# First stage of a hybrid encoder step: second projection ahead of the sixth tile's turn, and products of constants ahead of the first three turns

## What is computed

```
h = rms_norm(x, ln1);  proj = h @ w_in
q, k, v, f, xr, yg = split(proj)          # 8 heads of 64; f is one number per head and row
q = rms_norm(q, q_gain);  k = rms_norm(k, k_gain)
logf = log_sigmoid(f + b_f)
c = cumsum(logf)                          # per head, along the rows
s = q @ k^T / 8 + c[query] - c[key], causal;  attn = softmax(s) @ v
# a gated linear recurrence on xr, yg; w_out; then an MLP with squared relu
```

## Time and profile before

| | |
|---|---|
| median of 3 runs | 1388.46 us (1388.18 to 1390.19) |
| the profiled execution | 1392.37 us, its span 1390.7 us |
| mean granted clock of PE over the span | 0.994 |
| PE busy | 1351.1 us, 97% |
| DVE busy | 1038.5 us, 75% |
| ACT busy | 529.5 us, 38% |
| POOL busy | 391.4 us, 28% |

### The profile page before, as it was taken

The page is one execution under the profiler, slowest core; times in us unless marked ns, Lnnn a source line. Parts: engine busy times, 40 slices in busy tenths (PEclk is TensorE's granted clock), DMA queues, the critical chain, the costliest instruction groups (busy, mean ns, idle before and its releaser), DMA issues.

```text
span 1390.7 us, 21437 instructions
## 1 busy us (share of the span) xinstructions
PE 1351.1 (97%) x7399; PEld 1171.4 (84%) x7399; DVE 1038.5 (75%) x1610; ACT 529.5 (38%) x980; POOL 391.4 (28%) x397
## 2 busy tenths in 40 slices
PE   5999999999999998999999999999999999999998
PEld 4866948669589996889899999999999999999997
DVE  6775573745736687766888888888888888888885
ACT  6234252332436763324334333433442344234320
POOL 4411101111000030112354235423542453245310
PEclk9999999999999999999999999999999999999999
DMA  6042524324261212121211011102101110121004
GB/s 205 8 122 82 131 62 121 103 80 111 58 171 44 70 45 91 49 76 31 62 61 55 5 60 60 41 19 60 60 30 30 60 60 16 44 60 60 2 29 136
DMA packets 129544, 92.89 MB, mean 67 GB/s; under 512 B 14678, under 2 KB 119126, under 8 KB 129492
## 3 DMA queue, kind: packets, MB, share of 16 engines
q1 hardware_dynamic: 129492, 92.20, 23.0%
HBM read 78.28 MB, written 9.71 MB: 63 GB/s over the span
## 4 chain that ended last, share of the span: by engine, by line
PE 85%; DVE 6%; DMA 3%; ACT 2%; POOL 2%; issue 1%; SPq 1%; DVEq 0%; POOLq 0%; ACTq 0%
PE psum L2147 16%; PE psum L2148 16%; PE psum L2149 16%; PE psum L2644 8%; PE psum L2646 8%; PE psum L2645 8%; PE psum L2410 2%; DMA k_c<-in_cache_k_dram 2%; PE psum L2392 1%; PE psum L2230 1%; PE psum L2395 1%; PE psum L2363 1%; DVE tops L1673 1%; POOL rs L822 1%; DVE cross_qk L1660 1%
## 5 line engine op out<-in xcount | busy, mean ns | idle before, releaser
L2013 DVE TENSOR_TENSOR mix<-mix,psum 128x512 f32<-128x512 f32 x660 | 418.1, 685 | 91.5 <-PE psum L2646 87.2
L2147 PE MATMUL psum<-h_hi,wu_hi 128*128 128x384 f32 x768 | 259.5, 338 | 0.9 <-DVE wu_lo L1978 0.9
L2148 PE MATMUL psum<-h_lo,wu_hi 128*128 128x384 f32 x768 | 258.1, 336 | 0.0
L2149 PE MATMUL psum<-h_hi,wu_lo 128*128 128x384 f32 x768 | 258.1, 336 | 0.0
L2644 PE MATMUL psum<-wd_hi,u_hi 128*128 128x512 f32 x516 | 201.3, 390 | 0.1
L2645 PE MATMUL psum<-wd_lo,u_hi 128*128 128x512 f32 x516 | 200.7, 389 | 0.0
L2646 PE MATMUL psum<-wd_hi,u_lo 128*128 128x512 f32 x516 | 200.7, 389 | 0.0
L2147 PEld LDWEIGHTS psum<-h_hi,wu_hi 128*128 128x128 f32 x768 | 144.3, 188 | 10.0 <-issue 1.3
L2148 PEld LDWEIGHTS psum<-h_lo,wu_hi 128*128 128x128 f32 x768 | 144.3, 188 | 8.7
L2149 PEld LDWEIGHTS psum<-h_hi,wu_lo 128*128 128x128 f32 x768 | 144.4, 188 | 0.0
L1308 ACT CAST wd_hi<-raw 128x512 fp32r<-128x512 f32 x109 | 67.2, 623 | 179.5 <-PE psum L2646 81.1
(11 more groups left out here) (338 smaller groups left out, 2510.9 us busy)
## 6 DMA issues: line engine op xcount, KB each, us to landing
raw<-in_w_up_dram SPq DMA_DIRECT2D x32, 512.0 KB, 6.1
raw<-in_w_down_dram SPq DMA_DIRECT2D x32, 512.0 KB, 4.3
k_c<-in_cache_k_dram SPq DMA_DIRECT2D x32, 256.0 KB, 3.1
raw<-in_w_in_dram SPq DMA_DIRECT2D x32, 192.0 KB, 3.9
out_dram<-mix SPq DMA_DIRECT2D x9, 512.0 KB
v_c<-in_cache_v_dram SPq DMA_DIRECT2D x16, 256.0 KB, 4.4
raw<-in_w_in_dram SPq DMA_DIRECT2D x8, 512.0 KB, 4.1
raw<-in_w_out_dram SPq DMA_DIRECT2D x8, 512.0 KB, 4.2
```

The source lines that it names most:

```text
L2013: nc.vector.tensor_tensor(half_of(t, half), half_of(t, half), psum[:, product_bank(n), :].rearrange("p (k n) -> p k n", n=P), op).then_inc ...
L2147: nc.tensor.matmul(out, hi(k), r_hi(k), start=first and k == 0, stop=False)
L2148: nc.tensor.matmul(out, hi(k), r_lo(k), start=False, stop=False)
L2149: last = nc.tensor.matmul(out, lo(k), r_hi(k), start=False, stop=end and k == n - 1)
```

## The change

PE: 20, 10 and 20 turns of the identity into bank 3 (`warm`) stand ahead of the turns of tiles 0, 1 and 2; nobody reads them. `project(1)` stands right behind the turn of tile 4; what stood between (the turn of the small parameters, the turns of tiles 5 to 8, `forgets(0)` and `forgets(1)`) comes behind it, and the parameters are turned into bank 3 rather than 5. `forgets(2)` moves from behind `project(1)` into `project(2)`, `turn_inputs` from the first to the third quarter of `project(2)`, `turn_qk(0)` behind `project(2)`, `turn_forgets` from `project(3)` into `project(4)`.

DVE: `mean(1)` and `norm(1)` come among the tiles of the first stage; the series of logf is cut in two, with `norm(2)` between; both `prompt_sums` stand behind `norm(3)`, in halves with `prompt_rows`. SP: `keys_out(0, 2)` goes ahead of the rows of sums, which are written and read back in two halves. ACT, POOL: the same order as their new neighbours need.

```diff
@@ sync
-                if p == 0:
-                    sp.wait_ge(c_split, 1)
-                    sp.dma_start(c_dram[:, 0, :], c_row[0:H, :].bitcast(F32)).then_inc(c_saved, 16)
-                    sp.dma_start(c_dram[:, 1, :], c_row[32:32 + H, :].bitcast(F32)).then_inc(c_saved, 16)
-                    sp.wait_ge(c_saved, 32)
-                    sp.wait_ge(operands_set, 2)
-                    decay_rows(0)
...
                 keys_out(p, 2)
+                if p == 0:
+
+                    sp.wait_ge(operands_set, 2)
+                    for half in range(2):
+                        at = slice(half * SPAN, (half + 1) * SPAN)
+                        sp.wait_ge(c_split, half + 1)
+                        sp.dma_start(c_dram[:, 0, at], c_row[0:H, at].bitcast(F32)).then_inc(c_saved, 16)
+                        sp.dma_start(c_dram[:, 1, at], c_row[32:32 + H, at].bitcast(F32)).then_inc(c_saved, 16)
+                        sp.wait_ge(c_saved, 32 * half + 32)
+                        if half == 1:
+                            sp.wait_ge(c_rows_in, 32)
+                        decay_rows(0, at)
@@ vector
+                    if p == 0 and t == 2:
+                        first_stage(4)
+                        past_parts(1)
+                        forget_sizes()
...
-                    if p == 0 and t == 3:
-                        prompt_sums(1)
...
-                    if p == 0 and t == 0:
-                        first_stage(1)
+                    if p == 0 and t < 2:
+                        first_stage(2 * t + 1)
+                    if p == 0 and t == 2:
+                        forget_series()
                     norm(t)
-                    if p == 0 and t == 1:
-                        past_parts(1)
-                        forget_sizes()
+                    if p == 0 and t == 2:
                         forget_values()
-                    if p == 0 and t == 2:
-                        prompt_sums(0)
                     if p == 0 and t == 3:
-                        prompt_rows()
+                        for half in range(2):
+                            prompt_sums(half)
+                            prompt_rows(half)
                         own_sums()
@@ tensor
+            def warm(n):
+
+                for _ in range(n):
+                    nc.tensor.transpose(psum[:, f_bank(1), 0:P], ident[:], ident[:])
+
...
                     for t in range(3):
+                        warm((20, 10, 20)[t])
                         turn(t)
                 if i == 1:
                     turn(3)
                     turn(4)
+                if i == 2:
+                    turn(5)
                     pe.wait_ge(small_in, 16 * SMALL)
...
-                    turn(5)
                     forgets(0)
                     turn(6)
+                    pe.wait_ge(params_copied, 1)
                     forgets(1)
...
                 def amid(t, quarter):
-                    if p == 0 and (t, quarter) == (2, 0):
+                    if p == 0 and (t, quarter) == (2, 1):
+                        forgets(2)
+                    if p == 0 and (t, quarter) == (2, 2):
                         turn_inputs()
-                    if p == 0 and (t, quarter) == (3, 2):
+                    if p == 0 and (t, quarter) == (4, 2):
                         turn_forgets()
...
-                    if p == 0 and t == 1:
-                        forgets(2)
                     if p >= 1:
                         samples_meanwhile(p - 1, t)
-                    if 1 <= t < 8:
+                    if p == 0 and t == 2:
+                        turn_qk(0)
+                    if (1 if p >= 1 else 2) <= t < 8:
                         turn_qk(t - 1)
```

More of the change, by code:

```diff
@@ L862, in _ @@
             for t in range(5, NT):
+                if t == NT - 1:
+                    pair_rstd(0, 1)
                 x_rstd_of(t)
@@ L896, in _ @@
                         pool.wait_ge(shift_zeroed, 2 * p - 1 + hp)
-                for t in range(2 if p == 0 else 0, NT):
+                for t in range(3 if p == 0 else 0, NT):
                     pair_rstd(p, t)
@@ L1482, in first_stage @@
                 if i == 2:
-                    for t in (6, 7):
-                        x_mean_of(t)
-                        turn_lo(t - 2)
-                        x_norm(t)
+                    x_mean_of(6)
+                    turn_lo(4)
+                    x_norm(6)
+                    dve.wait_ge(rows_turned, 1)
+                    nc.vector.tensor_copy(param[:, :, 0:ROWS], psum[:, f_bank(1), 0:LC * ROWS].rearrange(
+                        "p (c r) -> p c r", c=LC)).then_inc(params_copied, 1)
+                    x_mean_of(7)
+                    turn_lo(5)
+                if i == 3:
+                    x_norm(7)
                     x_mean_of(8)
+                if i == 4:
                     x_norm(8)
@@ L1519, in forget_values @@
                 d.link(nc.vector.tensor_scalar(l_f[:], l_q[:], 1.0 / 15, None, ALU.mult))
-                for odd in (13, 11, 9, 7, 5, 3):
+                for odd in (13, 11, 9):
+                    d.link(nc.vector.scalar_tensor_tensor(l_f[:], l_f[:], 1.0 / odd, l_q[:], ALU.add, ALU.mult))
+            def forget_values():
+                for odd in (7, 5, 3):
                     d.link(nc.vector.scalar_tensor_tensor(l_f[:], l_f[:], 1.0 / odd, l_q[:], ALU.add, ALU.mult))
@@ L2352, in bound @@
                         pe.wait_ge(bound_read, 20 * p + BOUND_ORDER.index(BOUND_AFTER[hp, t]) + 1)
+                    if p == 0 and (hp, t) == (0, 1):
+                        pe.wait_ge(c_split, 2)
                     if (hp, t) == (0, 4):
+                        if p == 0:
+                            pe.wait_ge(c_rows_in, 64)
                         pe.wait_ge(lo_done, NT * p + 4)
```

27 lines of the change are left out of this document (12 added, 15 removed).

## The result

| kernel | median (lowest to highest), us | runs | to the kernel before, 95% interval |
|---|---|---|---|
| before | 1388.46 (1386.92 to 1390.19) | 7 | |
| after | 1392.31 (1389.55 to 1394.11) | 7 | 1.0028 [1.0018, 1.0037] |

The change made the kernel slower, by 3.9 us of 1388, clear of the noise but small; forecast was +0.6 us, with 1391.7 us as the end of the range. The profiled execution of the changed kernel took 1394.11 us (span 1392.4), that of before 1392.37 (1390.7).

What follows compares the result with a forecast made beforehand. PE and DVE hand work to and fro, neither alone the bound, with SP's queue third. A schedule shorter by 0.8 us and a clock fall of 1.4 us give +0.6 us: 1389.1 us, range 1384.6 to 1391.7.

Steps and rivals of the forecast that it cites:

- The stores hold `norm(3)`: On DVE, `norm(3)` waits 3.75 us for a key store queued on SP behind nine stores of logf.
- The landing is at 54.15 + 5.9: SP's first key store lands 5.9 us behind logf, at 60.05 us, and `norm(3)` waits for it.
- rival (C): Keys land sooner, so the stores don't hold DVE; `norm(3)` starts at 56.3 us: 1384.0 us, chance 0.17.
- Logf is ready at 54.15 us: On DVE, 27.4 us of work and 2.6 us of waits from 24.15 us make logf 3.1 us earlier.
- none for POOL's roots: DVE's waits for POOL's roots ahead of logf, before 0.72 and 1.55 us, vanish because other work lies between.
- the one for f: DVE waits some 0.65 us for f ahead of logf, because `forgets(2)` needs the lo part of tile 8.
- I take 0 us: The 50 turns of constants ahead of tiles 0 to 2 on PE change the time by 0 us, bounds +0.5 and -0.4.
- Rival (D): Clock falls around `turn(3)`, `project(1)` runs at half speed until some 31 us, logf 2.3 us late: 1391.4 us, chance 0.12.
- The fall behind 65 us: PE pauses 4 us behind `project(5)`, from 65.0 to 69.1 us, and the clock falls: 1.4 us lost, 1.2 to 2.4.
- The 0.3 us from the rows of sums: The first half of the sums is back from DRAM at 67.3 us, ahead of `norm(4)`, saving 0.3 us.
- From `norm(3)` to `norm(4)`: On DVE this stretch grows from 6.26 to 9.05 us by two running sums and rounding in halves.
- The base: The profile of before stood 3.9 us above the median, so +0.6 us was added to the median, 1388.46 us.

Runs made afterwards that it cites:

- Experiment 1: Changed kernel with the three key stores issued ahead of the nine stores of logf: 1387.57 us, 0.9999 of the kernel before.
- all_moves_no_products: Changed kernel without the 50 turns, key stores ahead of logf's, DVE's `qgain` product later, POOL's `e_row` built between the roots of x: 1389.20 us.
- experiment 7: Changed kernel with 16 more turns in two pauses (1390.81 us), with only the first 20 turns (1389.62), and reprofiled (1390.23); mean clocks compared with and without turns.
- after_again: The changed kernel, unchanged, profiled a second time: 1390.23 us (span 1388.5).
- no_products: Changed kernel without the 50 turns of the identity: 1389.07 us, 1.0004 of the kernel before.

## Why the prediction was wrong

The forecast was 1389.1 us in a range up to 1391.7, the time is 1392.31. By steps:

- **The stores hold `norm(3)`: right, and the largest single effect.** "The landing is at 54.15 + 5.9": the 5.9 us measured 5.97 (57.06 to 63.03). The wait was 4.86 us rather than 3.75, because DVE came to the wait 1.1 us behind logf (57.06 to 58.17) and not 2.15: I had counted 1.1 us for POOL's root ahead of the wait, and the root ran during it. Experiment 1 gives the price in time, 4.7 us; rival (C) had put 5.1 on it. This was forecast, so it is no part of the miss.
- **"Logf is ready at 54.15 us": wrong, 57.06,** and by more than the 1 us that the prediction had allowed. This term carries the miss at `norm(4)` (72.19 us, forecast 69.1). The 2.9 us are: 0.24 us later start (24.39 against 24.15); waits of 4.26 us (0.35, 1.57, 1.02, 0.85, 0.47) where I had 2.6, +1.66; and 28.4 us of work (57.06 - 24.39 - 4.26) where I had 27.4, +1.0. Of the waits, those up to the landing of the small parameters were 0.6 us longer (0.35 and 1.57 against 1.3), and I had written "none for POOL's roots" (0.85) and had none for ACT's squares (1.02, which came with the fall at 25 us); the one for f, 0.65, wasn't there. Of the work, `cc` and `c_mid`, moved beside POOL's building of `e_row`, took 3.06 us rather than 1.10. In the kernel before it was the instruction ahead of them that stood there:

```profile
44.56 1.10 DVE L1561 TENSOR_SCALAR c_past<-cc 64x512 bf16<-64x512 f32 x1
```

  It takes 0.42 us in the changed kernel, so that the net is +1.3 us, more than the whole +1.0. In the profiles without the fall at 25 us (`all_moves_no_products` and the kernels with the order of before aside) logf comes at 55.3 to 55.9 us, still 1.1 to 1.8 us late: the fall is 1.2 us of the miss, the rest is in every one of them.
- **"I take 0 us" for the constants' products: the step that failed.** My bounds were -0.4 and +0.5 us. They cost 3.2 us in the changed kernel, 2.6 us in the kernel before, 1.4 and 1.5 us in the two with the keys first. I had looked at what the turns delay, and not at what an earlier rise of the clock leads to. In its place the runs show that with the turns the clock is lower on average, by an estimated 1.1 to 2.1 us of PE's work (experiment 7), while the earlier end of `project(0)` only lengthens waits. One such fall is placed: behind the pauses ahead of tiles 3 and 4, in two of five profiles, and in none of the four of the same order without the turns. Rival (D) had this mechanism at 0.12, with 2.3 us on logf; measured 1.2 us on logf between two executions of one kernel.
- **The fall behind 65 us: right, but dearer in the text than on the chip.** I took 1.4 us. From norm(3) to norm(8) it takes 31.0 to 31.1 us in the seven profiles with the new order in which the clock falls in 70 to 75 us, and 30.3 us in the two in which it never falls in 60 to 80 us. It takes 30.3 us in `after_again` as well, where the fall came earlier, ahead of `norm(4)`:

```profile
60.00:65.00 5.00, 2.35 (x9) 2.33 (x9) 3.00 (x6) 2.05 (x5) 0.00 (x0) 0.76 0.18 44
65.00:70.00 5.00, 3.82 (x19) 3.50 (x18) 4.63 (x13) 1.36 (x4) 1.01 (x1) 0.90 0.08 15
```

  PE waits for `norm(4)` behind `project(5)` anyway, 2.26 us there and 3.79 in the first profile: the slower products took their time out of that wait. So a fall costs 0.8 us there or nothing, by where it lands. The 0.3 us from the rows of sums can't be seen.
- **From `norm(3)` to `norm(4)`** 9.16 us against 9.05: right.
- **The base.** The sum was moved to the median, and that was right: the profile of before had a fall at 304 us that its second profile hasn't (2.4 us of the fourth pair, 0.9 of them the longer wait).

Against the median, then: +0.6 forecast, +3.85 measured. Without the turns the changed kernel is at 1389.07 us: the forecast 1389.1 would have been that kernel's time, but in part by luck, with logf 1.1 us later than forecast and norm(8) 1.2 us later than before where 0.6 were forecast. In the medians, the whole miss is the size of the term that was priced at 0 (3.2 us, from 1389.1 to 1392.31); logf's other 1.1 us must be made good elsewhere, and I didn't find where, beyond the fall behind 65 us that was 0.6 us cheaper and the differences between executions behind norm(8).

**What stays open.** Of the 2.6 to 3.2 us that the turns cost in the kernel before and in the changed one, the traces place only part in the first pair: 0.2 to 0.6 us in the kernel before, and between `after_again` and `no_products` nothing at norm(8) (92.16 and 92.21), though the spans are 1.5 us apart. The traces do show where those 1.5 us arise. At 543.9 us the same products on PE are still 0.3 us apart, and at 547.3 us 1.5: the first kernel's clock falls there and the second's doesn't, behind a pause of 1.53 us in both. Windows of `after_again`, then of `no_products`:

```profile
545.00:550.00 5.00, 5.00 (x18) 3.92 (x18) 3.80 (x5) 1.80 (x4) 1.06 (x2) 0.77 0.02 3
```
```profile
545.00:550.00 5.00, 5.00 (x23) 4.03 (x22) 4.14 (x5) 1.47 (x4) 0.72 (x2) 1.00 0.00 0
```

Whether the turns make that fall more frequent isn't shown: it comes in seven of the eight profiles with all 50 turns and in six of the eight others. So how an act in the first 16 us could lower the mean clock, beyond the fall at 25 us and those behind 60 us, stays open.

Why the turns make the small parameters land later is open too; SP issues its loads within 0.2 us of the same times (the last group at 20.39 us in `after_again`, 20.20 in `no_products`), and that is less than the 0.5 to 1.0 us. One candidate stands in the traces and was not tested: a DMA queue that the profile calls `instruction` moves one block of 0.02 MB in this stretch. It starts at 20.7 to 24.8 us in the eight profiles with all 50 turns, in which the last small parameter lands at 26.5 to 27.1 us; at 25.8 us with 20 turns (26.3); and at 28.7 us or later, or not ahead of 30 us, in the seven without (26.0 to 26.1). It looks as if more instructions on PE brought that block forward, into the last small loads; that the one delays the other is argued from this order alone.

## What to carry to other kernels

An instruction that waits in a shared queue holds what stands behind it: before moving work that stands ahead of a wait, look whether that work was what covered it, and then first reorder the queue. An earlier issue of three stores was worth more than all moves of this change. Turns of constants are not free because nobody reads them: four pairs of kernels were slower with them, two of the four by more than their intervals. Raise the clock early only where the work behind is bound by PE and has no pauses (a case that no run here tested); here it was better left low until the products came. And one profile doesn't tell whether a fall of the clock belongs to a kernel: weigh it by the mean clock of all executions. Lastly, a ledger of one engine's work must price each operation beside its new neighbours, not its old ones.

## What the runs showed that I had not expected

DVE and POOL slow each other in some pairs of instructions on arrays in SBUF. On POOL, changed kernel, beside DVE's product of x at 35.80 to 37.08 us and then its work on `cc`:

```profile
25.15 1.02 POOL L827 TENSOR_TENSOR rs<-m,neg_half 128x4 f32<-128x4 f32 x1 [0.19 <-DVE m L1658]
...
36.04 1.93 POOL L827 TENSOR_TENSOR rs<-m,neg_half 128x4 f32<-128x4 f32 x1 [1.19 <-DVE m L1658]
...
44.94 1.67 POOL L878 TENSOR_SCALAR_AFFINE_SELECT build<-build 128x1024 f32<-128x1024 f32 x1
46.67 1.34 POOL L880 CAST e_row<-build 128x1024 bf16<-128x1024 f32 x1
```

The same root takes 1.02 us alone and 1.93 us there; `cc` takes 0.68 us alone and 1.92 beside the row at 44.94, `c_mid` 0.42 and 1.14 beside that at 46.67. The ends tell how: POOL's 44.94 ends at 46.61, and 0.68 more is 47.29, where `cc` ends at 47.11; POOL's 46.67 ends at 48.01, and 0.42 more is 48.43, where `c_mid` ends at 48.29. In `all_moves_no_products` POOL's 31.89 ends at 33.49, and 1.28 more is 34.77, where the product of x ends at 34.53. DVE's instruction takes nearly as long as if it began when POOL's ends. Not every neighbour does this: in the same kernel the product of x at 28.12 us runs beside a POOL memset (28.14 to 29.10 us) and takes 1.28 us. The Trainium skill (SBUF — State Buffer, section "Who interferes with whom") says that the two engines share a pair of ports, which one instruction holds as a whole while the other waits, and that DVE instructions with two inputs in SBUF, and casts, are among those that can want it. The trace agrees: `cc` and the product of x have two such inputs, `c_mid` is a cast, and each is held until about the end of one POOL instruction.

The second surprise is how much one execution differs from the next, with the same instructions in the same order: the changed kernel's two profiles are 3.9 us apart in span. Half of it, 2.0 us, is there at norm(8) of the first pair and comes from where the clock falls, 1.2 us at 25 us and 0.8 behind 70 us. The other half has nothing to do with the clock, which falls once more in each, by the same 1.7 us. Some 1.5 us of it are longer waits of PE for the cached keys. PE of the changed kernel's first profile, then of `after_again`, where the wait at the second of these places is gone:

```profile
219.14 1.39 PE L2258 MATMUL psum<-ident,k_c 128*128 128x128 f32 x8 [1.26 <-DMA k_c<-in_cache_k_dram]
...
394.29 0.66 PE L2258 MATMUL psum<-ident,k_c 128*128 128x128 f32 x4 [0.99 <-DMA k_c<-in_cache_k_dram]
```
```profile
216.64 1.39 PE L2258 MATMUL psum<-ident,k_c 128*128 128x128 f32 x8 [0.80 <-DMA k_c<-in_cache_k_dram]
```
